# Sliding attention and output block joined into one program per layer, in a two-layer decoder step on one Trainium2 core

## Chip, cores and metric

The kernel runs on one core of one Trainium2 chip. The metric is device microseconds (us) of one launch. The engines are TensorE (PE; its weight loads are listed as PEld), VectorE (DVE), ScalarE (ACT), GpSimd (POOL) and SyncE (SP), which issues the transfers spoken of here. Each runs its own queue in order and waits on semaphores.

## What is computed

Two decoder layers over 1032 tokens: a prompt of 1024 and 8 single samples. Cut to the part that the change touches (all in fp32):

```
proj = h @ w_in
attn = sliding-window attention (window 128, 8 q heads, 2 kv heads, head dim 64, per-head sink)
rec  = HGRN2 branch (4 heads, ready before this part begins)
x   += RMSNorm_post([attn ; rec] @ w_o)
hm   = rms_norm(mem_prompt) ; mk = hm @ w_xk ; mv = hm @ w_xv      # 256 memory rows, outputs too
q    = RMSNorm_pre(x) @ w_xq                                        # queries of the cross attention
```

After it come the cross attention, its output projection and the gated MLP; before it, the input projection and the recurrence.

## The kernel before

Everything is held transposed: `xT`, `Y`, `hh` and `hl` are [128, 8, 1032] in SBUF (channel blocks by tokens). A product keeps fp32 accuracy with three matmuls per block (`mm3`, lines 257 to 259): high part of the weights by high and by low part of the activations, and low part of the weights by the high part.

**Weights** come as slabs of 128x1024 (512 KB) in a fixed order of visits (`weight_visits`). A slab is loaded into one of RR = 2 raw buffers (`w_raw`, line 225), ACT rounds it to the high part (`w_hi`, line 234), and the low part is the difference, computed by POOL (line 242) or, for 13 slabs a layer (`LOW_ON_DVE`), by DVE (line 251). High and low parts have HR = 3 slots. The load of slab m waits for the low part of slab m-2; the high part of m waits until PE has used the slab whose slot it takes. `split_hi(act, upto)` in ACT's queue issues all high parts up to a number, each with its waits, and ACT's later work stands behind them. `fits_after(v)` is the number of slabs whose slot is free once v visits are done.

**stage_window** (line 379) computes the sliding attention in 16 groups g (8 query blocks of 128, two halves of the heads). A group on PE is `scores(g+3)` (line 447), one slab of the memory's keys and values (`memory(g)`), `turn(g+1)` (transposes of the shares, line 457) and `values(g)` (line 470). DVE does `before(g+2)` (scale and mask line 588, maximum 595, small ones 596 to 598), `after(g+1)` (603 to 606), the memory's result (611) and the low part of the attention's output (580). ACT does the exponentials (526), the copy of the transposes (535), the copies of the turned memory values (557) and `split_hi`. The memory's products share bank 7 of PSUM, so each waits for the result before it.

**stage_output_query** (line 1288) is a program of its own. All engines meet between the two. It computes 24 units of the output projection (`wo`) and 24 of the queries (`xq`). A unit is one block of 128 output channels by one third of the tokens (384, 384 or 264 wide, `C3`), 24 matmuls. The order of `wo` is: for each k, thirds 0 and 1 (units 0 to 15), then third 2 for k = 7 down to 0 (units 16 to 23). ACT squares and copies each result (`evacuate`, 1478 and 1481), DVE sums the squares (1553). Of each third follow a mean on PE (1386), a root on ACT (1488), a reciprocal (1565) and `normalise` (1572) on DVE, `residual` (1579), then `high` on ACT (1494), `low` on DVE (1589), ACT's squares of the new x (1506) with their sums, and the reciprocal `scale` (1598). The two buffers `sq` make ACT wait for the sum two before. Third 0 is finished while units 16 to 23 run, thirds 1 and 2 while queries run. PE starts the first query after the copy of unit 23 (`out` >= 24). The eight samples' attention is threaded between units 1 and 16. The residual x comes back from memory in one transfer (line 1350).

## Time and profile before

| | |
|---|---|
| median of 3 runs | 3636.25 us (3630.45 to 3642.39) |
| profiled execution: its own time | 3634.12 us |
| profiled execution: span, first to last instruction | 3632.3 us |
| PE busy | 3359.7 us, 92% of the span |
| DVE busy | 2360.1 us, 65% |
| ACT busy | 1193.9 us, 33% |
| POOL busy | 677.1 us, 19% |

The part in question stands twice in the span, once for each layer: from 421.4 us to about 769.6 us in layer 0, and 1800 us later with nearly the same waits in layer 1. Busy shares are averages over stages with different limits; the order of the instructions in one stage tells more.

### The profile page before, as it was taken

The page shows a single profiled execution, that of the slowest core. Times are in us where ns is not written, and L with a number is a line of the kernel's source. Part 1 is how long each engine was busy: PE and PEld are TensorE (multiplying, and loading weights), DVE is VectorE, ACT ScalarE, POOL GpSimd, SP SyncE. Part 2 cuts the span into 40 slices and gives each one's busy share as a digit, 9 for nine tenths or more (in the row PEclk, how much of TensorE's full clock was granted, in tenths as well). Part 3 has the DMA queues.
Part 4 walks back from the last instruction along what each step waited for, and adds up shares of the span by engine and source line. Part 5 has one row for each costly group of instructions (what it writes and reads, how often), then busy time and mean ns, then how long its engine had stood idle before and what let it go on. Part 6 is the DMA issues. An engine that isn't in the chain of part 4 may idle for free. (4 is left out here: it accounts for less than half of the span.)

```text
span 3632.3 us, 49879 instructions
## 1 busy us (share of the span) xinstructions
PE 3359.7 (92%) x20860; PEld 3139.7 (86%) x20860; DVE 2360.1 (65%) x3509; ACT 1193.9 (33%) x1849; POOL 677.1 (19%) x274
## 2 busy tenths in 40 slices
PE   6999789889999999999989997798899999999997
PEld 6999768778599999999879996698786999999996
DVE  6776781824276777767787777737334676776766
ACT  5342362424232222222344424533333322212222
POOL 1111132011132122121111111311122212122120
PEclk8999899999999999999999998999999999999998
DMA  4111223212421111111121122322033111111111
GB/s 163 42 42 63 69 82 117 76 47 76 174 68 47 42 53 44 44 47 42 56 75 40 48 65 67 105 105 70 30 130 143 56 41 53 41 47 47 41 53 54
DMA packets 67807, 245.74 MB, mean 68 GB/s; under 512 B 7936, under 2 KB 19456, under 8 KB 62208
## 3 DMA queue, kind: packets, MB, share of 16 engines
q1 hardware_dynamic: 67008, 242.32, 19.6%
q8 instruction: 165, 2.70, 0.3%
q14 instruction: 58, 0.48, 0.0%
q10 hardware_dynamic: 576, 0.24, 0.0%
HBM read 214.20 MB, written 23.04 MB: 65 GB/s over the span
## 5 line engine op out<-in xcount | busy, mean ns | idle before, releaser
L257 PE MATMUL ps<-hh,w_hi 128*128 128x344 f32 (+2 forms) x4320 | 1420.6, 329 | 112.2 <-issue 26.0
L259 PE MATMUL ps<-hh,w_lo 128*128 128x344 f32 (+2 forms) x4320 | 1392.8, 322 | 0.0
L258 PE MATMUL ps<-hl,w_hi 128*128 128x344 f32 (+2 forms) x4320 | 1392.4, 322 | 0.0
L242 POOL TENSOR_TENSOR w_lo<-w_raw,w_hi 128x1024 fp32r<-128x1024 f32 x270 | 676.9, 2509 | 2892.7 <-ACT w_hi L234 2892.7
L257 PEld LDWEIGHTS ps<-hh,w_hi 128*128 128x128 f32 x4320 | 823.8, 191 | 150.1 <-issue 94.0
L258 PEld LDWEIGHTS ps<-hl,w_hi 128*128 128x128 f32 x4320 | 823.9, 191 | 2.5 <-issue 0.2
L259 PEld LDWEIGHTS ps<-hh,w_lo 128*128 128x128 f32 x4320 | 823.1, 191 | 0.0
L2540 DVE TENSOR_TENSOR Y<-Y,ps 128x344 f32<-128x344 f32 x912 | 432.9, 513 | 156.1 <-PE ps L259 156.1
L234 ACT ACTIVATE w_hi<-w_raw 128x1024 fp32r<-128x1024 f32 x296 | 310.8, 1052 | 464.1 <-PE ps L259 397.0
L2336 ACT ACTIVATE f_c<-f_u,cT 128x1032 f32<-128x1032 f32 (+1 forms) x92 | 111.4, 1213 | 669.9 <-DVE f_u L2505 663.3
L259 PE MATMUL ps<-f_ghi,w_lo 128*128 128x344 f32 x960 | 307.8, 321 | 0.0
L257 PE MATMUL ps<-f_ghi,w_hi 128*128 128x344 f32 x960 | 306.2, 319 | 0.0
L258 PE MATMUL ps<-f_glo,w_hi 128*128 128x344 f32 x960 | 306.0, 319 | 0.0
L2513 DVE SCALAR_TENSOR_TENSOR f_c<-f_u,cT,f_c 128x1024 f32<-128x1024 f32 x172 | 225.2, 1309 | 98.8 <-ACT f_c L2336 95.8
L258 PEld LDWEIGHTS ps<-f_glo,w_hi 128*128 128x128 f32 x960 | 180.8, 188 | 0.0
L259 PEld LDWEIGHTS ps<-f_ghi,w_lo 128*128 128x128 f32 x960 | 180.2, 188 | 0.0
L257 PEld LDWEIGHTS ps<-f_ghi,w_hi 128*128 128x128 f32 x960 | 180.2, 188 | 0.0
L2505 DVE TENSOR_TENSOR f_u<-ps,rs 128x1032 f32<-128x1032 f32 x86 | 105.7, 1229 | 99.1 <-PE ps L259 98.8
L2515 DVE SCALAR_TENSOR_TENSOR f_c<-f_cache,cT,f_c 128x8 f32<-128x8 f32 x172 | 123.7, 719 | 6.2
L1553 DVE TENSOR_TENSOR oq_acc<-oq_acc,oq_sq 128x384 f32<-128x384 f32 (+1 forms) x84 | 43.3, 515 | 97.1 <-ACT oq_sq L1478 92.9
L1084 DVE TENSOR_TENSOR Y<-ps,rs 128x344 f32<-128x344 f32 x120 | 60.1, 509 | 53.5 <-PE ps L259 53.3
L2352 ACT ACTIVATE f_ghi<-f_c 128x1032 fp32r<-128x1032 f32 x42 | 44.9, 1068 | 149.3 <-DVE f_c L2521 149.3
(352 smaller groups left out, 3963.8 us busy)
## 6 DMA issues: line engine op xcount, KB each, us to landing
w_raw<-in_w_stream SPq DMA_DIRECT2D x296, 512.0 KB, 3.3
out_y_cols<-xT SPq DMA_DIRECT2D x9, 1376.0 KB, 6.3
xT<-out_y_cols SPq DMA_DIRECT2D x2, 4128.0 KB, 15.7
mem_keys<-in_cache_mem_k SPq DMA_DIRECT2D x8, 1024.0 KB, 4.8
mem_values<-in_cache_mem_k SPq DMA_DIRECT2D x8, 1024.0 KB, 5.0
mem_keys<-in_cache_mem_v SPq DMA_DIRECT2D x8, 1024.0 KB, 4.8
mem_values<-in_cache_mem_v SPq DMA_DIRECT2D x8, 1024.0 KB, 5.0
xT<-in_x_cols SPq DMA_DIRECT2D x1, 4128.0 KB, 14.9
```

The costliest lines, as they stand in the source:

```text
L234: nc.scalar.activation(w_hi[:, SLOT[m], :], w_raw[:, m % RR, :], ACT.Copy).then_inc(hi_done, 1)
L242: nc.gpsimd.tensor_tensor(w_lo[:, SLOT[m], :], w_raw[:, m % RR, :], w_hi[:, SLOT[m], :].bitcast(F32), ALU.subtract).then_inc(lo_done["pool ...
L257: nc.tensor.matmul(out, whi, mhi, start=start, stop=False)
L258: nc.tensor.matmul(out, whi, mlo, start=False, stop=False)
L259: return nc.tensor.matmul(out, wlo, mhi, start=False, stop=stop)
L1084: nc.vector.tensor_tensor(dst[:, cols(c)], ps[:, u % 3, 0:CH], rs[:, cols(c)], ALU.mult)\
L2336: nc.scalar.activation(C[:, h, at], U[:, h, 2 + at.start:2 + at.stop], ACT.Identity, bias=cT[:, l, 3, col:col + 1], scale=cT[:, l, 2, col: ...
L2352: nc.scalar.activation(gh[:, j % 2, :], C[:, 1, :], ACT.Copy).then_inc(f_gh, 1)
L2505: nc.vector.tensor_tensor(tokens3(U[:, h, 2:2 + T]), ps[:, 3 * h:3 * h + 3, 0:CH], tokens3(rs[:]), ALU.mult).then_inc(f_up, 1)
L2513: dve_c(nc.vector.scalar_tensor_tensor(c[:, 0:SEQ], U[:, h, t:t + SEQ], w, c[:, 0:SEQ], ALU.mult, ALU.add))
L2515: dve_c(nc.vector.scalar_tensor_tensor(c[:, SEQ:T], ca[:, col, t, :], w, c[:, SEQ:T], ALU.mult, ALU.add))
L2540: nc.vector.tensor_tensor(y, y, b, ALU.add).then_inc(f_y, 1)
```

## The change

The two programs become one, `stage_window_output`. Its parts:

- The group loop takes two memory slabs in each of groups 0 to 7 (`memory(2g+1)` and `memory(2g+2)`, with `memory(0)` before the first turn), and one or two `wo` units in groups 8 to 15 (`UNITS_OF`), units 0 to 10 in all. Units 0 to 11 share bank 7 of PSUM.
- `wo` runs third by third: k = 0..7 for third 0, 7..0 for third 1, 0..7 for third 2. That is a third visit, and five more slabs to load and split in each layer, on POOL. The 13 slabs of `LOW_ON_DVE` stay 13: they are k = 3 to 7 of third 2 and the eight of `xq`.
- High parts are asked for one group earlier (`fits_after(visit + 1)`).
- ACT does the exponentials before the copy of the turned memory values.
- Third 0 is normalised and added to x during units 11 to 15, before unit 16; third 1 is normalised, added, squared and split while units 17 to 23 run. The squares of both new thirds are threaded between the copies of units 18 to 23 (`SQUARES`).
- x comes back in three transfers, one for each third, with slab loads between them. The two caches of the samples and the sinks are asked for after the memory's last product.

```
+    v += [(("wo", k, 2), S_WO + k) for k in range(KT)]
...
-              if VISIT[l, "wo", KT - HR, 1] < LOAD_OF.index(m) < VISIT[l, "xq", KT - 1, 1]]
+              if VISIT[l, "wo", HR - 1, 2] < LOAD_OF.index(m) < VISIT[l, "xq", KT - 1, 1]]
...
+                o_passes = [(k, 0) for k in range(KT)] + [(k, 1) for k in reversed(range(KT))] + [(k, 2) for k in range(KT)]
+                UNITS_OF = [[]] * 8 + [[0], [1], [2], [3], [4], [5, 6], [7, 8], [9, 10]]
+                MEANS = [("post", 0), ("post", 1), ("pre", 0), ("pre", 1), ("post", 2), ("pre", 2)]
...
                     def _(sp):
+                        load_slabs(sp, LOAD_OF[VISIT[l, "mem", KT + 4]])
+                        sp.wait_ge(s["t_out"], 4)
+                        sp.dma_start(io["mem_v"][l], mv).then_inc(mem_stored, 16)
+                        load_slabs(sp, LOAD_OF[VISIT[l, "wo", 1, 0]])
+                        sp.wait_ge(s["m_out"], N_MEMW)
+                        sp.dma_start(io["mem_k"][l], cT2[:]).then_inc(mem_stored, 16)
+                        sp.wait_ge(w_used, VISIT[l, "wo", 0, 0])
                         sp.dma_start(kcT[:], io["cache_win_k"][l]).then_inc(kv_in, 16)
                         sp.dma_start(vc[:], io["cache_win_v"][l]).then_inc(kv_in, 16)
...
-                        load_slabs(sp, LOAD_OF[VISIT[l, "wo", 4, 0]] + 1)
-                        sp.wait_ge(kept, 1)
-                        sp.dma_start(xT[:], io["y_cols"]).then_inc(x_in, 16)
+                        load_slabs(sp, LOAD_OF[VISIT[l, "wo", 3, 1]] + 1)
+                        sp.wait_ge(s["kv_out"], 32)
+                        sp.wait_ge(s["pv"], n)
+                        sp.wait_ge(dve_did, KEPT)
+                        for c in range(NCH):
+                            sp.dma_start(xT[:, :, cols(c)], io["y_cols"][:, :, cols(c)]).then_inc(x_in[c], 16)
+                            load_slabs(sp, LOAD_OF[VISIT[l, "wo", 3, 1]] + 2 * c + 3)
...
+                        memory(0)
+                        turn(0)
+                        for g in range(n):
+                            if g + 3 < n:
+                                scores(g + 3)
+                            if 1 <= g <= 4:
+                                turn_values(g - 1)
+                            if g < KT:
+                                memory(2 * g + 1)
+                            else:
+                                unit("wo", UNITS_OF[g][0])
+                            if g + 1 < n:
+                                turn(g + 1)
+                            if g < KT - 1:
+                                memory(2 * g + 2)
+                            for u in UNITS_OF[g][1:]:
+                                unit("wo", u)
+                            values(g)
+                            if g == n - 2:
+                                sample_scores()
+                        mean(0)
+                        unit("wo", 11)
                         sample_rows()
+                        unit("wo", 12)
                         sample_probs()
+                        unit("wo", 13)
+                        unit("wo", 14)
                         sample_values()
+                        unit("wo", 15)
                         unit("wo", 16)
                         mean(1)
+                        for u in range(17, 22):
                             unit("wo", u)
+                        mean(2)
+                        unit("wo", 22)
+                        unit("wo", 23)
+                        unit("xq", 0)
+                        mean(3)
+                        unit("xq", 1)
+                        mean(4)
+                        for u in range(2, 9):
                             unit("xq", u)
...
+                            if 1 <= g <= 4:
+                                act.wait_ge(s["t_done"], g)
...
+                            if g < KT:
+                                split_hi(act, fits_after(VISIT[l, "mem", 2 * g] + 1))
+                                if g < RH:
+                                    rows_high(g)
+                                split_hi(act, fits_after(VISIT[l, "mem", 2 * g + 1] + 1))
+                            else:
+                                if g < KT + RH:
+                                    rows_high(g - RH)
+                                evacuate(UNITS_OF[g][0])
+                                split_hi(act, fits_after(visit("wo", UNITS_OF[g][0]) + 1))
+                            if g + 1 < n:
+                                copy(g + 1)
+                            for u in UNITS_OF[g][1:]:
+                                evacuate(u)
                                 split_hi(act, fits_after(visit("wo", u) + 1))
+                        out_high(NB - 1)
+                        root(0)
+                        evacuate(11)
...
+                        root(1)
+                        high(0)
+                        for u in (17, 18):
+                            evacuate(u)
+                            split_hi(act, fits_after(visit("wo", u) + 1))
+                        squares(0, range(4))
+                        evacuate(19)
+                        split_hi(act, fits_after(visit("wo", 19) + 1))
+                        squares(0, range(4, KT))
+                        evacuate(20)
+                        split_hi(act, fits_after(visit("wo", 20) + 1))
+                        high(1)
+                        evacuate(21)
...
+                        act.wait_ge(x_ready, 2)
+                        squares(1, range(4))
+                        evacuate(22)
+                        split_hi(act, fits_after(visit("wo", 22) + 1))
+                        squares(1, range(4, KT))
+                        evacuate(23)
...
                         low_slab(0)
-                        normalise(0)
+                        normalise(1)
                         add_post(17)
                         low_slab(1)
-                        residual(0, range(0, 4))
+                        low(0, range(KT))
                         add_post(18)
                         low_slab(2)
-                        residual(0, range(4, 8))
+                        residual(1, range(4))
+                        add_pre(0, range(1, 4))
                         add_post(19)
                         low_slab(3)
-                        low(0, range(0, 4))
+                        residual(1, range(4, KT))
+                        add_pre(0, range(4, KT))
                         add_post(20)
                         low_slab(4)
-                        low(0, range(4, 8))
                         add_post(21)
                         low_slab(5)
+                        scale_of(2)
+                        low(1, range(4))
+                        add_pre(1, range(1, 4))
                         add_post(22)
+                        low(1, range(4, KT))
+                        add_pre(1, range(4, KT))
                         add_post(23)
                         low_slab(6)
-                        root(1)
-                        normalise(1)
+                        query(0)
                         low_slab(7)
-                        add_pre(0)
```

`mean`, `unit`, `evacuate`, `scores`, `turn`, `values`, `before` and `after` keep their instructions; their waits follow the new order.

## Rows read from the trace of the kernel before

**Rows 1.** The page's first line.

```profile
span 3632.3 us, 49879 instructions
```

**Rows 2.** Waits of PE over the whole span: total us, times, longest.

```profile
PE ps L457 <- DVE xT L606: 37.7, 24, 7.3
...
PE ps L257 <- DVE w_lo L251: 25.4, 12, 5.3
...
PE ps L257 <- ACT mem_values L557: 7.1, 8, 0.9
```

**Rows 3.** Windows of layer 0: busy us of each engine, granted clock, DMA share.

```profile
436.00:500.00 64.00, 56.87 (x432) 45.24 (x430) 56.57 (x87) 45.30 (x108) 16.72 (x7) 0.98 0.18 58
...
640.00:700.00 60.00, 47.48 (x278) 44.97 (x278) 51.64 (x69) 29.16 (x52) 0.00 (x0) 0.93 0.28 93
...
657.91:663.20 5.29, 5.29 (x24) 5.29 (x24) 3.89 (x7) 1.06 (x1) 0.00 (x0) 0.50 0.39 126
```

**Rows 4.** Timeline of PE, layer 0: start, us, wait before it.

```profile
556.25 0.66 PE L257 MATMUL ps<-hh,w_hi 128*128 128x384 f32 x1 [7.48 <-PEq L416]
...
657.91 0.59 PE L257 MATMUL ps<-hh,w_hi 128*128 128x264 f32 x1 [5.34 <-DVE w_lo L251]
...
664.41 0.41 PE L257 MATMUL ps<-hh,w_hi 128*128 128x384 f32 x1 [0.85 <-ACT Y L1481]
```

**Rows 5.** Timeline of POOL in the window loop.

```profile
470.89 2.39 POOL L242 TENSOR_TENSOR w_lo<-w_raw,w_hi 128x1024 fp32r<-128x1024 f32 x1 [5.18 <-ACT w_hi L234]
```

**Rows 6.** Timeline of DVE in the window loop.

```profile
468.31 1.21 DVE L588 SCALAR_TENSOR_TENSOR xT<-ps,swa_mask 128x1024 f32<-128x1024 f32 x1
...
471.01 2.29 DVE L597 TENSOR_TENSOR win_small<-sinks,win_small 128x4 f32<-128x4 f32 x1
```

**Rows 7.** Timeline of ACT: one exponential of four; its last small one.

```profile
473.54 0.51 ACT L526 ACTIVATE xT<-xT,win_small 128x256 f32<-128x256 f32 x1 [2.73 <-DVE win_small L598]
...
476.08 0.20 ACT L528 ACTIVATE win_small<-win_small 128x4 f32<-128x4 f32 x1
```

**Rows 8.** Timeline of SP between the two programs.

```profile
555.34 0.43 SPq L429 DMA_DIRECT2D out_mem_k<-mem_keys  x1
...
556.59 1.83 SPq L1345 DMA_DIRECT2D ws_values<-in_cache_win_v  x1
...
559.28 0.44 SPq L1350 DMA_DIRECT2D xT<-out_y_cols  x1
```

**Rows 9.** Issues of transfers, 500 to 575 us: KB each, us to landing.

```profile
w_raw<-in_w_stream SPq DMA_DIRECT2D x10, 512.0 KB, 3.2
...
xT<-out_y_cols SPq DMA_DIRECT2D x1, 4128.0 KB, 15.5
```

**Rows 10.** Timeline of ACT in the output projection.

```profile
609.50 0.49 ACT L1478 ACTIVATE oq_sq<-ps 128x384 f32<-128x384 f32 x1 [2.39 <-PE ps L259]
...
613.70 0.49 ACT L1478 ACTIVATE oq_sq<-ps 128x384 f32<-128x384 f32 x1 [3.33 <-PE ps L259]
...
634.08 0.39 ACT L1478 ACTIVATE oq_acc<-ps 128x264 f32<-128x264 f32 x1 [0.78 <-PE ps L259]
...
650.00 4.14 ACT L1494 ACTIVATE hh<-xT,gT 128x384 fp32r<-128x384 f32 x8
```

**Rows 11.** Timeline of DVE, unit 16 to the last query.

```profile
633.33 2.55 DVE L1565 RECIPROCAL oq_rt<-oq_rt 128x384 f32<-128x384 f32 x1 [1.72 <-ACT oq_rt L1488]
...
635.92 1.23 DVE L251 TENSOR_TENSOR w_lo<-w_raw,w_hi 128x1024 fp32r<-128x1024 f32 x1
...
637.07 3.35 DVE L1572 TENSOR_TENSOR Y<-Y,oq_rt 128x3072 f32<-128x3072 f32 x1
...
641.94 2.20 DVE L1579 SCALAR_TENSOR_TENSOR xT<-Y,gT,xT 128x384 f32<-128x384 f32 x4
...
672.62 4.53 DVE L1553 TENSOR_TENSOR oq_acc<-oq_acc,oq_sq 128x384 f32<-128x384 f32 x7
...
769.54 0.43 DVE L1608 TENSOR_TENSOR Y<-ps,rs 128x264 f32<-128x264 f32 x1 [2.35 <-PE ps L259]
```

More of the change, by code:

```diff
@@ L1360, in _, with scores @@
                     def _(pe):
+                        def scores(g):
+                            if g >= 2:
+                                pe.wait_ge(s["scores_used"], g - 1)
+                            b, jp = divmod(g, 2)
+                            k0 = P * (b - 1) if b else 0
+                            sv = scores_of(g)
+                            for j in range(2):
+                                for kv in range(NKV):
+                                    rows = slice(HD * kv, HD * kv + HD)
+                                    last = nc.tensor.matmul(sv[:, 2 * kv + j, keys_of(g):], qT[rows, 2 * jp + j, P * b:P * b + P],
+                                                            kT[rows, k0:P * (b + 1)], start=True, stop=True)
+                            last.then_inc(s["scores"], 1)
@@ new lines, in turn @@
+                        def turn(g):
+                            pe.wait_ge(s["probs"], g + 1)
+                            if g:
+                                pe.wait_ge(s["turned_copied"], g)
+                            for half in halves_of(g):
+                                for h in range(4):
+                                    last = nc.tensor.transpose(ps[:, 4 + half, P * h:P * h + P],
+                                                               S[g % 3][:, 256 * h + P * half:256 * h + P * half + P], ident[:])
+                            last.then_inc(s["turned"], 1)
@@ new lines, in values @@
+                        def values(g):
+                            b, jp = divmod(g, 2)
+                            pe.wait_ge(s["turned_copied"], g + 1)
+                            if b and jp == 0:
+                                pe.wait_ge(s["out_used"], b)
+                            pt = PT[g % 2].rearrange("p (a h q) -> p a h q", a=2, h=4)
+                            hs = halves_of(g)
+                            for i, half in enumerate(hs):
+                                for kv in range(NKV):
+                                    last = nc.tensor.matmul(ps[HD * kv:HD * kv + HD, 6, 256 * jp:256 * jp + 256],
+                                                            vtok[:, b - 1 + half, HD * kv:HD * kv + HD],
+                                                            pt[:, half, 2 * kv:2 * kv + 2].rearrange("p h q -> p (h q)"),
+                                                            start=(i == 0), stop=(i == len(hs) - 1))
+                            last.then_inc(s["pv"], 1)
@@ L1536, in _ @@
                         high(2)
-                        squares(2)
+                        squares(2, range(KT))
                         split_hi(act, fits_after(VISIT[l, "xq", 7, 0] + 1))
-                        root(4)
                         root(5)
@@ new lines, in _ @@
+                        after(0)
+                        for g in range(n):
+                            if g + 2 < n:
+                                before(g + 2)
+                            if g < KT:
+                                memory(2 * g)
+                            if g and g % 2 == 0:
+                                out_low(g // 2 - 1)
+                            if g + 1 < n:
+                                after(g + 1)
+                            if 1 <= g <= RH:
+                                rows_low(g - 1)
+                            elif KT < g <= KT + RH:
+                                rows_low(g - RH - 1)
+                            if g < KT:
+                                memory(2 * g + 1)
+                            for u in UNITS_OF[g]:
+                                if u % KT:
+                                    add_post(u)
@@ L1622, in _ @@
+                        out_low(NB - 1)
+                        dve.wait_ge(pe_did, ROWS)
                         sc = HD ** -0.5
@@ L1680, in _ @@
-                        query(0)
+                        scale_of(3)
                         query(1)
-                        residual(1, range(0, 4))
+                        normalise(4)
+                        query(2)
                         low_slab(9)
-                        query(2)
-                        residual(1, range(4, 8))
+                        residual(2, range(4))
                         query(3)
                         low_slab(10)
-                        root(3)
```

695 lines of the change are left out of this document (292 added, 403 removed).

## The prediction, made before the changed kernel was run

> **What bounds the kernel now.** I read the page first, then PE's waits, then windows of layer 0, then the timelines of each queue around the waits. The profiled execution took 3634.12 us of its own time, 1.8 us more than its span [rows 1]; it lies 2.1 us under the median 3636.25. PE is busy for 92% of the span, so a change like this can win only PE's waits. Those that it touches [rows 2, 4], halved for one layer: the turns wait for the shares, 18.9 us, of which 7.3 at the first turn and 11.5 in the loop; 3.6 behind the copies of the memory values; 7.5 between the two programs; 12.7 for low parts made by DVE. Two windows say why [rows 3]. In 436 to 500 us DVE works 56.57 of 64 us, as much as PE: the loop is at DVE's limit. In 640 to 700 us DVE works 51.64 of 60 us and PE only 47.48: here DVE sets the pace.
>
> **The clock.** After the wait of 5.34 us PE ran at half clock (0.50, the 1.2 GHz level) for 5.3 us [rows 3, 4], which costs 2.65 us. I charge this wherever a wait is longer than that and PE sets the pace afterwards; the wait of 7.5 between the programs pays it too.
>
> **Step 1, what goes, per layer.** The meeting of all engines: 7.5 + 2.6 = 10.1 us. The turns' waits in the loop, 11.5: a group of the first eight gives PE two memory products in place of one. PE's own work in a group: 432 matmuls in 64 us at 44 a group are 9.8 groups, 56.87 / 9.8 = 5.8 us each [rows 3]; a unit of 384 columns is 4.2 us by the spacing of its squares [rows 10], a memory product of 256 columns 4.2 x 256/384 = 2.8; so 3.0 are the group's own and the new group has 3.0 + 5.6 = 8.6 us. DVE's part grows only by one more result. The copies' waits, 3.6. The first memory product ahead of the first turn: about 1.2, since it waits only for the memory's low parts. Sum: -26.4 us.
>
> **Step 2, what comes in the window loop and units 0 to 15.**
> (a) In groups 1 to 4 ACT now does exponentials before it copies the turned values, and the product behind waits. Exponentials last 2.7 us [rows 7] and start when DVE has the maxima, after one 1.2 us pass, one about as long and three small ones [rows 6]. So the copy, some 0.5 like a unit's [rows 10], is ready about 0.4 + 3.1 + 2.7 + 0.5 = 6.7 us after a product, when PE has the group's 3.0, a product of 2.8 and four transposes, about 0.6, behind it, 6.4: wait 0.3. If POOL's low part stands in the way of DVE's small instruction, add 2: the one at 471.01 took 2.29 us and ended with POOL's [rows 5, 6]. Two slabs a group make that frequent. I take 1.5 of 0.3 to 2.3, four times: 6 us (1 to 9).
> (b) SyncE's queue has slab k=1 of the output projection behind the memory's last result, the store of the keys, and the caches. From the store to what follows the caches SyncE took 3.9 us [rows 8]. Count from the end of the last memory product: result 0.5, queue 3.9, landing 3.2 alone [rows 9], or about 4.6 behind 2 MB of store and caches at 4.2 MB in 15.5 us and the rest; so 7.6 to 9. ACT, a group ahead, stands at this slab and the next before the copy of turn 8, so that both high parts (1.9), copy (1.0), the attention's output high and low (1.1) and DVE's shares (1.6) follow: 13.2 to 14.6. PE comes to the turn that wants the shares after 3.0 + 4.2 = 7.2. Wait 6 to 8.7; I take 8.7, as the caches really are in front, and half clock after it: 11.3 us.
> (c) The same at slab k=2 of third 1: it is issued after the last `values`, behind 1.6 MB of x, and lands 7 us later. ACT stands at it before the last attention output and the first root. High part, output high and low: 9.5. PE has a mean and unit 11, 5.1, then unit 12 waits 4.4; with half clock 7.0 (0 to 8).
> (d) Units 0 to 10 share one bank, with one group's own work between: its copy, 0.9, is hidden behind 3.0, unless ACT is late. A group with one unit has 7.2 us of PE against DVE's same 7. I take 0.3 a group, 2.3 us. The five more slabs (ACT 1.06, POOL 2.4 each) lie in these gaps; a further price would be the shared port, in (a).
> Sum of 2: +26.6. Steps 1 and 2 cancel: +0.2 (range -9 to +8).
>
> **Step 3, third 2 of the projection.** Count from the end of unit 16, T. PE has a mean 0.6 and five units of 4.2 x 264/384 = 2.9: 15.1 us, then `mean(2)`, which wants all sums of new third 0. DVE's queue before that: the root is there at T+3.4 (evacuation 0.7, high part 1.0, mean and root 1.7, as before the reciprocal at 633.33), then reciprocal 2.55, normalise 3.35, low parts of third 0 4.3, three slabs after the first 3.5, half of `residual` twice 4.3, seven sums of squares 4.5, three more sums 1.2 [rows 11]. End: T+27. PE waits 12.
> Then ACT: copy of unit 20, a high part, `high(1)` 4.1 [rows 10], unit 21's copy; 6.4 in all, and DVE goes on: slab, `scale` 2.55, low 4.3, seven sums 4.5 less what ACT runs ahead, two sums, and ACT copies unit 23, which stands behind its last squares. I count 12.6 to 14. So T+46 (to 48) for query 0, against 15.1 + 0.6 + 5.8 = 21.5 of PE's work. Before, from unit 16's end at 634.0 to the first query at 664.4 [rows 4, 10]: 30.4. Thus +15.6 us. The half clock is inside these waits, for DVE sets the pace.
>
> **Step 4, the queries.** Before: 664.4 to 769.5, 105.1 us [rows 4, 11]. PE's work: 16 x 4.2 + 8 x 2.9 + means 1.6 = 92.1. After, DVE has less left (`scale` twice, root and normalise of third 2, residual and low of third 2, eight sums, seven slabs, nine results: 31 us) under nine queries of 38 us. I leave 6 us of waits for the order, half of the 13, and 2.6 of half clock: 100.8. -4.3; between 0 and -10.
>
> **The sum.** +0.2 + 15.6 - 4.3 = +11.5 a layer, twice: 3634.1 + 23.0 = 3657.1 us, +0.6%; the 2.1 us between this execution and the median lie inside the range. Everything else of the span keeps its instructions.
>
> **A rule beside the rows.** At 471.01 DVE ended with POOL [rows 5, 6]. The Trainium skill, "SBUF — State Buffer", Who interferes with whom, says that DVE with two SBUF inputs and POOL exclude each other for whole instructions. The trace agrees. By it alone two slabs a group could cost DVE 4.8 us in each of eight groups, and the time would be rival 3's.
>
> **Rivals.**
> 1. Faster: DVE's queue in third 2 is not the limit (place: between unit 16 and query 0). For it: before, the same engines finished third 0 there with one long wait of 5.3. Against: DVE's list above, 27 us before `mean(2)` alone. If the stretch takes 30.4 as before, the sum is 0.2 - 4.3 = -4.1 a layer, and with (b) at 6 + 2.6, its low end, -6.8: 3634.1 - 13.6 = 3620 us. It decides once the stretch is under some 34 us. The Trainium skill, "Perfetto Trace Analysis", Optimization Strategy, says that interleaving regimes with different busiest engines may help; by it this rival would hold. The loop does interleave so, and third 2 is the opposite.
> 2. The slabs of (b) and (c) cost half of their waits, 4 and 2 us, and no half clock: 6 in place of 18.3. Step 3 stays: -0.8 a layer, 3632.5 us. No change. For it: 3.2 us of landing alone. Against: SyncE's order, which nothing shortens.
> 3. The port: DVE loses 2.4 us for each slab in the eight groups with two slabs and is the bound: 56.57 / 9.8 = 5.8 [rows 3] + 4.8 = 10.6 against PE's 8.6, 16 us in eight groups less the 6 that (a) has: +10 on the forecast, 3657 + 20 = 3677 us. Against: in 436 to 500 us seven slabs by POOL (16.72 us) left DVE 7 us of room [rows 3], and part of its passes read PSUM.
> 4. The change does not do what it says: the meeting stays, as a chain of the same waits. That is (b), and is in the forecast.
>
> **Chances.** Forecast, with its own range 3645 to 3672: 0.58. Rival 1: 0.15. Rival 2: 0.13. Rival 3: 0.10. 0.04 for something else. A difference under 0.3%, 11 us, can hardly be told from none. Faster takes rival 1; same takes rival 2 and the forecast's lowest end; the rest is slower: 0.16, 0.15, 0.69. The range that holds 8 in 10 leaves a tail of rival 1 and of rival 3: 3624 to 3684.
>
> **What the profile after would show.** Step 1: no wait of 7.5 before unit 0, waits of turns in groups 1 to 8 under 1 us in all. 2a: four waits of 0.3 to 2.3 for `mem_values`. 2b: one wait of 6 to 9 at turn 9, ACT before it waiting for a transfer. 2c: about 4 before unit 12. Step 3: PE's busy share from unit 17 to query 0 under 55%, with DVE near 90%. Step 4: waits under 9 us in the queries. I would be wrong if ACT passes slab k=1 without a wait, or if query 0 starts under 34 us after unit 16.

## The result, and the profile after

The changed kernel took 3669.22 us (median of 4, 3663.34 to 3674.97) against 3634.62 us for the kernel before beside it: a ratio of 1.0097, interval 1.0084 to 1.011, or 34.6 us more. The forecast was 3657 us, 23 us more, in a range of 3624 to 3684. The profiled execution below is the longest of the four (3674.97 us, span 3673.1), 5.8 us above their median, so sums over its trace come out larger by that.

The waits of TensorE after; the columns are as in [rows 2]:

```profile
PE ps L258 <- issue: 60.4, 44, 11.4
PE ps L1174 <- DVE xT L1539: 22.6, 6, 10.1
...
PE ps L258 <- ACT mem_values L1437: 15.7, 8, 2.4
PE ps L258 <- DVE w_lo L252: 15.4, 6, 3.3
...
PE ps L258 <- DVE hl L1513: 12.9, 2, 6.5
PE ps L1254 <- DVE oq_acc L1559: 12.4, 2, 6.2
...
PE ps L2051 <- PEq L1119: 8.8, 2, 4.4
```

The turns' 24 waits of 37.7 us are 6 of 22.6, and of these two are 10 us long. The copies of the memory values cost 15.7 us instead of 7.1. A new wait for `hl` (line 1513, the attention output's low part) stands before unit 12, one for `oq_acc` before `mean(2)`, and what the profile calls "issue" has a new longest of 11.4. Where they lie is in the timeline of TensorE after, layer 0; it answers to [rows 4]:

```profile
451.78 0.36 PE L258 MATMUL ps<-mem_hi,w_hi 128*128 128x256 f32 x1 [2.37 <-ACT mem_values L1437]
...
476.50 0.36 PE L258 MATMUL ps<-mem_hi,w_hi 128*128 128x256 f32 x1 [0.91 <-ACT mem_values L1437]
...
537.15 1.12 PE L1174 MATMUL ps<-ident,xT 128*128 128x128 f32 x4 [10.10 <-DVE xT L1539]
...
619.37 0.66 PE L258 MATMUL ps<-hh,w_hi 128*128 128x384 f32 x1 [6.47 <-DVE hl L1513]
...
670.72 1.01 PE L1254 MATMUL ps<-oq_acc,ones 128*128 128x384 f32 x1 [6.20 <-DVE oq_acc L1559]
...
690.32 0.66 PE L258 MATMUL ps<-hh,w_hi 128*128 128x384 f32 x1 [11.31 <-issue]
...
797.72 0.76 PE L2051 MATMUL ps<-mem_keys,Y 128*128 128x256 f32 x1 [4.41 <-PEq L1119]
```

From top to bottom: two of the four waits for the copies; turn 9; unit 12; `mean(2)`; query 0; the cross attention. Windows of the changed kernel, layer 0 (busy us of PE, PEld, DVE, ACT, POOL; then the granted clock):

```profile
448.00:460.00 12.00, 9.28 (x64) 8.57 (x60) 6.11 (x11) 6.43 (x14) 4.76 (x2) 0.86 0.29 94
460.00:470.00 10.00, 7.75 (x50) 6.75 (x50) 4.26 (x11) 5.81 (x14) 2.39 (x2) 0.83 0.29 85
...
537.00:543.00 6.00, 5.85 (x30) 4.02 (x31) 5.79 (x10) 4.08 (x10) 2.35 (x1) 0.67 0.38 132
619.00:625.00 6.00, 5.63 (x23) 5.66 (x24) 2.91 (x12) 5.07 (x9) 3.84 (x2) 0.68 0.66 224
643.00:670.00 27.00, 17.14 (x122) 16.31 (x120) 23.57 (x31) 15.81 (x30) 0.00 (x0) 0.89 0.24 78
670.00:690.00 20.00, 8.29 (x50) 7.47 (x50) 14.71 (x23) 13.35 (x28) 0.00 (x0) 0.76 0.16 53
690.00:696.00 6.00, 5.68 (x22) 5.71 (x23) 1.68 (x3) 1.17 (x2) 0.00 (x0) 0.62 0.23 87
```

Each long wait is followed by some us at a clock between the two levels of 1.2 and 2.4 GHz on average (0.67, 0.68, 0.62), and the loop's short waits by 0.86 and 0.83. In third 2 TensorE works 25.4 of 47 us while VectorE works 38.3.

To see in which stretch the time went, I put four events of a layer on one scale. Zero is SyncE's load of `mem_cols`, with which the window's program begins; "mem" is the time between the first and the last result of a memory product, "last mem" when the last one comes, "unit 16" is ScalarE's first work on its result, "cross" the first matmul of the cross attention (us, layer 0 / layer 1; the edits follow below):

| kernel | mem | last mem | unit 16 done | cross |
|---|---|---|---|---|
| before | 107.1 / 107.1 | 126.5 / 126.4 | 212.8 / 212.6 | 356.7 / 356.2 |
| after | 81.3 / 81.3 | 98.2 / 98.0 | 221.4 / 221.0 | 376.2 / 376.1 |
| e1 | 79.6 / 81.0 | 96.4 / 96.9 | 208.4 / 208.7 | 362.9 / 363.2 |
| e2 | 79.6 / 77.7 | 96.5 / 93.5 | 213.6 / 208.3 | 367.7 / 361.6 |
| e3 | 73.4 / 73.1 | 90.3 / 89.7 | 214.7 / 213.4 | 369.4 / 368.8 |
| e5 | 77.7 / 79.5 | 93.7 / 96.3 | 218.4 / 218.5 | 340.4 / 341.1 |
| e6 | 73.1 / 73.1 | 89.0 / 89.0 | 194.8 / 193.4 | 347.9 / 347.4 |
| e7 | 73.5 / 73.1 | 90.3 / 89.8 | 194.8 / 194.2 | 316.3 / 315.6 |
| e8 | 77.8 / 77.8 | 93.6 / 93.6 | 218.3 / 215.6 | 377.3 / 374.3 |

In layer 0 of the kernels before and after, the change loses 8.6 us up to the end of unit 16 and 10.8 behind it. The loss behind it is +17.0 from unit 16 to query 0 (47.4 us, 642.93 to 690.32, against 30.4), -2.1 for the queries (103.0 against 105.1) and -4.1 at the meeting before the cross attention (4.41 us; the kernel before waits 8.55 there). After, e1, e2, e5 and e8 have the same code between the two memory events and differ by up to 3.6 us there. That much is the clock of one execution: TensorE's 546 matmuls of this stretch take 69.5 to 72.9 us in these ten layers, while its idle time in it is nearly the same, 8.2 to 8.7 us. The 81.3 of the changed kernel's profiled execution is 2.0 above the mean of the ten, 79.3.

### The profile page after: what moved, and what is told of

Same layout as the page of the kernel before. It is cut to its first block and busy times, and to the rows that moved or that the text cites. A ratio compares the mean times of both kernels' runs of the same rounds, so it can differ in the third digit from the quotient of the medians.

```text
span 3673.1 us, 49999 instructions
## 1 busy us (share of the span) xinstructions
PE 3375.6 (92%) x20860; PEld 3158.3 (86%) x20860; DVE 2347.9 (64%) x3517; ACT 1205.8 (33%) x1871; POOL 697.9 (19%) x284
## 3 DMA queue, kind: packets, MB, share of 16 engines
q1 hardware_dynamic: 74400, 247.56, 19.9%
## 5 line engine op out<-in xcount | busy, mean ns | idle before, releaser
L243 POOL TENSOR_TENSOR w_lo<-w_raw,w_hi 128x1024 fp32r<-128x1024 f32 x280 | 697.7, 2494 | 2912.7 <-ACT w_hi L235 2912.7
L235 ACT ACTIVATE w_hi<-w_raw 128x1024 fp32r<-128x1024 f32 x306 | 321.9, 1053 | 575.4 <-PE ps L260 452.9
L258 PE MATMUL ps<-mem_hi,w_hi 128*128 128x256 f32 x256 | 80.9, 316 | 28.0 <-ACT mem_values L1437 15.7
```

The source lines that it names most:

```text
L235: nc.scalar.activation(w_hi[:, SLOT[m], :], w_raw[:, m % RR, :], ACT.Copy).then_inc(hi_done, 1)
L243: nc.gpsimd.tensor_tensor(w_lo[:, SLOT[m], :], w_raw[:, m % RR, :], w_hi[:, SLOT[m], :].bitcast(F32), ALU.subtract).then_inc(lo_done["pool ...
L258: nc.tensor.matmul(out, whi, mhi, start=start, stop=False)
```

## The experiments

Eight kernels were run. Gains are given as ratios to the kernel before beside them; a difference of two ratios times 3634.6 us is the gain in us. For the changed kernel the ratio is 1.0097.

**e1, slabs before the store.** One line of SyncE:

```diff
-                        load_slabs(sp, LOAD_OF[VISIT[l, "wo", 1, 0]])
+                        load_slabs(sp, LOAD_OF[VISIT[l, "wo", 3, 0]])
                         sp.wait_ge(s["m_out"], N_MEMW)
                         sp.dma_start(io["mem_k"][l], cT2[:]).then_inc(mem_stored, 16)
```

> The changed kernel with one edit: SyncE issues slabs k=1 and k=2 of the output projection's third 0 before it stores the memory's keys and loads the caches, instead of after. In the changed kernel's layer 0 the slab is issued at 523.12 us, behind the store (520.18) and the caches, although POOL had made its buffer free at about 513; ACT stands at it for 10.91 us and TensorE waits 10.10 us at turn 9. Theory (SyncE's order costs it): the slab lands before the last memory product is done, the wait of 10.10 us at turn 9 goes in both layers, and with it about 2 us of half clock after it: 20 to 26 us less than the changed kernel's 3669, so 3643 to 3649. Rival (the slab is late whoever is first, because a group ahead is too early for two raw buffers): a wait of 5 us or more stays at turn 9, and the time is 3657 or above.

Measured: 3647.98 us, ratio 1.0037 (1.0023 to 1.005): 22 us less than the changed kernel. SyncE's timeline of the changed kernel, with ScalarE's wait for the slab behind it:

```profile
520.18 0.34 SPq L1133 DMA_DIRECT2D out_mem_k<-mem_keys  x1
...
522.00 1.07 SPq L1137 DMA_DIRECT2D ws_sinks<-in_attn_sinks  x1
523.12 1.01 SPq L226 DMA_DIRECT2D w_raw<-in_w_stream  x2
...
529.82 1.06 ACT L235 ACTIVATE w_hi<-w_raw 128x1024 fp32r<-128x1024 f32 x1 [10.91 <-DMA w_raw<-in_w_stream]
```

and the same queue in e1, with the window that had a clock of 0.67 in the changed kernel (e1's turn 9 runs earlier, at 521.95, and its clock is 1.00 in each window of 6 us from 515 to 545):

```profile
501.37 9.37 SPq L226 DMA_DIRECT2D w_raw<-in_w_stream  x3
514.86 0.34 SPq L1133 DMA_DIRECT2D out_mem_k<-mem_keys  x1
...
537.00:543.00 6.00, 6.00 (x42) 4.93 (x41) 4.85 (x10) 3.95 (x9) 2.40 (x1) 1.00 0.01 3
```

In e1 the three slab loads are issued before the store, and the six waits of turns are 3.2 us in all, the longest 1.0, where they were 22.6 and 10.1. So the slab was late because of its place in the queue, and the rival is out. From the last memory result to unit 16 e1 needs 112.0 / 111.8 us where the changed kernel needs 123.2 / 123.0: 11.2 us a layer, of which 9.7 are the turns' waits and the rest, by difference, the clock.

**e2, slabs before x.** SyncE loads two slabs of third 1 more before it waits for the last values and loads x:

```diff
-                        load_slabs(sp, LOAD_OF[VISIT[l, "wo", 3, 1]] + 1)
+                        load_slabs(sp, LOAD_OF[VISIT[l, "wo", 3, 1]] + 3)
...
-                            load_slabs(sp, LOAD_OF[VISIT[l, "wo", 3, 1]] + 2 * c + 3)
+                            load_slabs(sp, LOAD_OF[VISIT[l, "wo", 3, 1]] + 2 * c + 5)
```

> The changed kernel with one edit: two slabs of third 1 more are issued before SyncE waits for the last values and loads x, so that no slab is queued behind x (1.5 MB each for the first two thirds). In the changed kernel's layer 0 ACT stands at such a slab for 9.47 us until 616.96, and TensorE waits 6.47 us before unit 12, with a granted clock of 0.68 in the 6 us after it. Theory (the slab is late because it is behind x in the queue): the wait of 6.5 us goes in both layers with up to 3 us of slow clock: 13 to 19 us less than 3669, so 3650 to 3656. Rival (third 2 is set by VectorE's queue, which starts no earlier): the wait goes from unit 12 but returns before the first query, and the time stays within 4 us of 3669.

Measured: 3655.89 us, ratio 1.0053 (1.004 to 1.0066): 16 us less. TensorE no longer waits for `hl` of line 1513. In the changed kernel that wait came by way of ScalarE, which stood at the slab:

```profile
616.96 1.06 ACT L235 ACTIVATE w_hi<-w_raw 128x1024 fp32r<-128x1024 f32 x1 [9.47 <-DMA w_raw<-in_w_stream]
```

From the last memory result to unit 16 it needs 117.1 / 114.8 us, 7.2 a layer less than the changed kernel. From unit 16 to the cross attention it needs 154.1 / 153.3 against 154.8 / 155.1: the gain does not return in third 2, against the rival.

**e3, copies first.** In ScalarE's loop the copy of the turned memory values moves from behind `exps(g + 2)` to ahead of it and of `out_high`:

```diff
+                            if 1 <= g <= 4:
+                                act.wait_ge(s["t_done"], g)
+                                nc.scalar.activation(mv..., ps[:, 7, :]..., ACT.Copy).then_inc(s["t_out"], 1)
                             if g and g % 2 == 0:
                                 out_high(g // 2 - 1)
                             if g + 2 < n:
                                 exps(g + 2)
```

> The changed kernel with one edit: in groups 1 to 4 ACT copies the turned memory values before it does the exponentials, as the kernel before does, not after them. The changed kernel has four waits of TensorE there, 2.37, 2.25, 0.91 and 2.25 us = 7.8 us in layer 0, and the granted clock is 0.83 to 0.86 in 448 to 470 us and 0.50 in 490 to 493 us. Theory (ACT's order, and short waits one behind another bring the clock down too): the four waits are about 0.9 each as before, 4 us less, and the clock is 1.00 there, 3 to 5 us less: 7 to 9 a layer, 14 to 18 in all, so 3651 to 3655. Rival A (only the waits count; the slow clock has another cause): 8 us less, 3661, with the clock as it was. Rival B (the exponentials now come later, so that the turns wait for the shares instead): no gain, and waits of the turns in groups 1 to 5 of 0.5 us or more.

Measured: 3659.92 us, ratio 1.0061 (1.0048 to 1.0075): 13 us less by the ratios, 9.3 by the medians. The intervals are too wide to tell the theory's 14 from rival A's 8; the trace tells more. Waits of TensorE and windows of e3:

```profile
PE ps L258 <- ACT mem_values L1433: 6.2, 8, 0.8
...
448.00:460.00 12.00, 10.86 (x89) 9.69 (x88) 9.12 (x14) 7.15 (x16) 6.25 (x4) 1.00 0.28 89
460.00:470.00 10.00, 8.64 (x70) 7.46 (x70) 7.92 (x12) 6.13 (x15) 3.77 (x2) 1.00 0.32 105
```

The eight waits go from 15.7 to 6.2 us, 4.75 a layer; the clock is 1.00 where it was 0.86 and 0.83, and no waits of turns come in (22.2 in 6, against 22.6), so rival B is out. The stretch between the memory results is 73.2 us, against a mean of 79.3 over the ten layers with the other order (table): 6.1 us a layer. How much of it is clock can be read from the 546 matmuls that every one of these stretches has; here are the changed kernel, e5 (which has its order) and e3:

```profile
438.41:519.73 81.32, 72.87 (x546) 64.08 (x545) 50.59 (x82) 46.35 (x105) 33.26 (x14) 0.94 0.27 91
```

```profile
435.34:513.07 77.73, 69.56 (x546) 60.86 (x545) 50.31 (x82) 46.34 (x105) 33.27 (x14) 0.98 0.28 96
```

```profile
441.99:515.39 73.40, 68.60 (x546) 59.55 (x545) 55.19 (x81) 45.87 (x105) 33.11 (x14) 1.00 0.31 101
```

TensorE is idle for 4.8 us in e3 and for 8.3 on the mean of the ten: 3.5 less, since about 1.1 of the 4.75 come back as waits for a memory result. Its matmuls take 68.4 us against a mean of 71.0: 2.6 are clock. Both parts of the theory hold, and rival A is out by the trace, but the clock's part was not the same each time, 1.1 to 4.4 us a layer, with a mean below the 3 to 5 I expected.

**e4, clears earlier.** This is the kernel before with one line moved:

```diff
-                        load_slabs(sp, fits_after(end) + RR)
-                        sp.wait_ge(mem_stored, 32 * (l + 1))
-                        clear(sp, "hg", "w")
+                        load_slabs(sp, fits_after(end) + RR - 2)
+                        clear(sp, "hg", "w")
+                        load_slabs(sp, fits_after(end) + RR)
+                        sp.wait_ge(mem_stored, 32 * (l + 1))
```

> The kernel before with one edit: SyncE clears the 65 semaphores of the earlier programs before it issues the last two slabs of the output block's program, not after them. The changed kernel waits 4.41 us before the cross attention, the kernel before 8.55 us; nothing else there differs but where semaphores are cleared, and SyncE took 2.58 us from the load ahead of 43 clears to the store behind them in the changed kernel. Theory (the clears are on the path at the meeting of engines, 0.06 us each): 65 x 0.06 = 3.9 us a layer less, the wait before the cross attention about 4.5, and 3634.6 - 8 = 3627 us. Rival (the longer wait is something else, for example the weights' high part): no change, 3634, and the wait stays above 8 us.

Measured: 3625.25 us, ratio 0.9973 (0.9962 to 0.9985): 9.4 us less than the kernel before. The timeline of the kernel before shows SyncE's last load and then TensorE's wait to the cross attention:

```profile
773.10 0.33 SPq L225 DMA_DIRECT2D w_raw<-in_w_stream  x1
...
778.06 0.76 PE L2024 MATMUL ps<-mem_keys,Y 128*128 128x256 f32 x1 [8.55 <-PEq L1341]
```

In e4 the same wait is

```profile
771.02 1.19 PE L2025 MATMUL ps<-mem_keys,Y 128*128 128x256 f32 x2 [4.41 <-PEq L1341]
```

In the 4.6 us between SyncE's last load (773.10 + 0.33) and 778.06 nothing of SyncE is in the trace: clears leave no record. In the changed kernel 44 clears lie between these two rows of SyncE:

```profile
421.56 0.34 SPq L1122 DMA_DIRECT2D mem_values<-in_mem_cols  x1
424.48 0.34 SPq L1126 DMA_DIRECT2D out_win_k<-xT  x1
```

424.48 - 421.56 - 0.34 is 2.58 us for 44, 0.06 us each; the kernel before makes 66 at its meeting (by one each more than I had counted for the expectation). The wait is 4.1 us shorter with nothing moved but the clears, and the rival is out. So the 4.1 us a layer that the changed kernel wins at this meeting come from where it clears semaphores, not from joining the programs.

**e5, sums after queries.** Third 2 of the changed kernel in another order. TensorE, and the order of sums and means:

```diff
-                MEANS = [("post", 0), ("post", 1), ("pre", 0), ("pre", 1), ("post", 2), ("pre", 2)]
+                MEANS = [("post", 0), ("post", 1), ("pre", 0), ("post", 2), ("pre", 1), ("pre", 2)]
+                SQUARES = [(kind, c, i) for kind in ("post", "pre") for c in range(NCH) for i in range(KT)]
...
-                                pe.wait_ge(out, 24)
+                                pe.wait_ge(out, min(24, 21 + u))
...
-                        for u in range(17, 22):
-                            unit("wo", u)
-                        mean(2)
...
+                        for u in range(17, 24):
+                            unit("wo", u)
+                        for u in range(24):
+                            if u in (3, 4, 10, 12):
+                                mean({3: 2, 4: 3, 10: 4, 12: 5}[u])
+                            unit("xq", u)
```

ScalarE evacuates units 17 to 23 in a row and then does the squares of third 0, roots 2 and 3, `high(1)`, `high(2)`, the squares of third 1, root 4, the squares of third 2 and root 5, with the slabs' high parts between them. VectorE's queue up to query 8 is now: slab 0, `normalise(1)`, slabs 1 and 2, the sums of units 17 to 23 with `low(0)`, slabs 3 to 6 and the first half of `residual(1)` between them, slab 7, the sums of new third 0, the second half of `residual(1)`, slabs 8 and 9, `scale_of(2)`, queries 0 and 1, slab 10, `normalise(3)`, slab 11, queries 2 to 4, slab 12, query 5, `residual(2)`, `low(1)`, `low(2)`, the sums of third 1, queries 6 and 7, the sums of third 2, `scale_of(4)`, query 8, `scale_of(5)`. The operations are the same ones.

> The changed kernel with the order of third 2 changed and nothing else: VectorE makes the sums of squares of the new thirds, their roots' reciprocals and the low parts of third 1 after what the first query wants; ScalarE evacuates units 17 to 23 before it squares the new thirds; TensorE does its means between queries 3 and 12, and a query waits only for the evacuation of its own bank. In the changed kernel 47.4 us lie between the end of unit 16 and query 0, against 21.5 us of TensorE's work, and VectorE works 38.3 of them. Theory (VectorE's queue in third 2 sets the pace, and about 20 us of its work are not wanted by the first query): query 0 starts 23 to 30 us after unit 16, some of it comes back as waits between queries 4 and 9, and the time falls by 10 to 20 us a layer: 3629 to 3649. Rival A (VectorE's whole work up to query 9 sets the end): the first query comes early, but the last query is less than 5 us a layer earlier, 3659 or above. Rival B (the chain through ScalarE, not VectorE's work, holds query 0): it starts 40 us or more after unit 16.

Measured: 3604.56 us, ratio 0.992 (0.9904 to 0.9936): 64 us less than the changed kernel, where I had expected 20 to 40, and less than the kernel before. The first row is TensorE's query 0 in e5 (unit 16 was done at 637.84), the others are windows of e5, unit 16 to query 0 and query 0 to the cross attention; the next fence has the same two windows of the changed kernel:

```profile
660.58 0.44 PE L258 MATMUL ps<-hh,w_hi 128*128 128x384 f32 x1
...
637.84:660.50 22.66, 21.16 (x170) 20.49 (x168) 18.68 (x21) 16.42 (x31) 0.00 (x0) 1.00 0.34 116
660.50:759.80 99.30, 93.91 (x585) 91.98 (x585) 57.32 (x93) 35.97 (x62) 19.07 (x8) 0.99 0.24 80
```

```profile
642.93:690.30 47.37, 25.50 (x172) 23.80 (x171) 38.48 (x54) 29.53 (x59) 0.00 (x0) 0.83 0.21 67
690.30:797.70 107.40, 97.83 (x582) 96.59 (x583) 38.33 (x59) 22.31 (x34) 19.08 (x8) 0.94 0.21 69
```

Query 0 starts 22.7 us after unit 16 instead of 47.4, and both rivals are out. VectorE does the same work in all, 76.0 against 76.8 us, but only 18.7 us of it before query 0 instead of 38.5. TensorE has 6.9 us without work instead of 31.4, and its own matmuls take 115.1 us instead of 123.3, because the clock stays up: of the 32.8 us a layer, 24.6 are waits and 8.3 the clock. The edit reorders three queues at once and lets the first queries wait for fewer evacuations; no run moves VectorE's queue alone, so what each part is worth stays open.

**e6, three orders.** The edits of e1, e2 and e3 together.

> The changed kernel with the edits of e1, e2 and e3 together. Theory (three waits at three places that don't hide one another): the gains add, 21.2 + 13.3 + 9.3 = 43.8 us, 3625. Rival (VectorE or ScalarE then sets the pace between the places, so that part of one gain is lost in another): 3635 or above, with new waits of TensorE between turn 9 and unit 12.

Measured: 3616.86 us, ratio 0.9955 (0.9942 to 0.9968): 52 us less than the changed kernel; the three alone gave 22 + 16 + 13 = 51 by the same reckoning. They add within their intervals, and the rival is out. The median is below the 3625 expected because that sum took the medians' smaller differences, 43.8. The joined program now reaches unit 16 at 194.8 / 193.4 us, 18.6 a layer earlier than the kernel before.

**e7, four orders.** The edits of e1, e2, e3 and e5 together.

> The changed kernel with the edits of e1, e2, e3 and e5 together. Theory: the gain of e5 (20 to 40 us) comes on top of the 44 of the other three: 3585 to 3605, below the kernel before (3634.6) by 0.8 to 1.4%. Rival (with units 0 to 16 done earlier, VectorE and POOL are what the queries wait for): the gain of e5 is halved or lost, 3610 to 3625.

Measured: 3551.98 us, ratio 0.9778 (0.9765 to 0.9792): 2.2% faster than the kernel before, 116 us less than the changed kernel; e5 and e6 add up to 64 + 52. It is better than even the theory had it, since e5 gave more than the 20 to 40 us I had put down. VectorE and POOL do not become what the queries wait for: from unit 16 to the cross attention it needs 121.5 / 121.4 us, e5 122.0 / 122.6.

**e8, five lows twice.** In the changed kernel VectorE makes the low parts of the five slabs of third 2 twice:

```diff
                         def low_slab(i):
+                            if i < 5:
+                                m = LOW_ON_DVE[len(LOW_ON_DVE) // DEPTH * l + i]
+                                dve.wait_ge(hi_done, m + 1)
+                                dve_c(nc.vector.tensor_tensor(w_lo[:, SLOT[m], :], w_raw[:, m % RR, :],
+                                                              w_hi[:, SLOT[m], :].bitcast(F32), ALU.subtract))
                             split_lo_dve(dve, LOW_ON_DVE[len(LOW_ON_DVE) // DEPTH * l + i] + 1)
```

> The changed kernel with VectorE making the low parts of the five slabs of third 2 twice (the same values written again, 1.2 us each): a price put on VectorE's queue between units 17 and 23. Theory (VectorE sets the pace there): 5 x 1.2 = 6 us later at query 0 in each layer, 12 us in all, 3681. Rival A (ScalarE's chain sets it and VectorE has room, 9 of 47 us idle): under 4 us in all, 3669 to 3673. Rival B (the extra work keeps POOL off the shared port too): over 16 us, 3685 or more.

Measured: 3678.19 us, ratio 1.0124 (1.0106 to 1.0142): 10 us more than the changed kernel. The two intervals overlap (the changed kernel's ends at 1.011), so the times alone can't tell the theory's 12 from rival A's 4, or from no change; the trace does. Query 0 of e8:

```profile
695.74 0.66 PE L258 MATMUL ps<-hh,w_hi 128*128 128x384 f32 x1 [11.47 <-issue]
```

Unit 16 was done at 644.07, so it starts 51.7 us after it, 4.3 more than in the changed kernel for 6.2 us of added work; in layer 1 it is 4.3 too. VectorE's queue sets the pace there, with about 2 us of slack where it waits for ScalarE (its wait of 3.09 us for the square of unit 21 is 1.83 in e8). Rival A's 4 us in all would be 2 a layer, and rival B's 16 would be 8.

## Why the prediction was right, and where its sizes were off

The direction and the mechanism were right: what the joined program wins in the loop it loses again at three places, and the order of third 2 makes it slower. By the table the change costs 19.5 and 19.9 us a layer where I had 11.5; by the medians it is 17.3. That the sum came this near is in part luck: the steps were 8.3, 1.4 and 2.2 us too low, and 4.1 came back at a place that had no term.

**Steps 1 and 2, up to unit 16: +0.2 forecast, +8.5 measured.** The windows from SyncE's load of `mem_cols` to unit 16 have the same 1259 matmuls in each kernel. Before:

```profile
421.30:634.08 212.78, 182.70 (x1259) 159.85 (x1260) 120.36 (x198) 108.05 (x246) 51.16 (x21) 0.94 0.27 93
```

after:

```profile
421.56:642.93 221.37, 186.33 (x1259) 164.31 (x1260) 123.65 (x211) 113.32 (x255) 61.79 (x26) 0.91 0.30 101
```

and e6:

```profile
424.64:619.44 194.80, 179.30 (x1259) 158.01 (x1260) 129.26 (x211) 112.60 (x255) 62.68 (x26) 0.96 0.31 110
```

On the mean of both layers TensorE idles 30.0 us before, 34.6 after and 15.6 in e6, and its matmuls take 182.7, 186.6 and 178.5. So the +8.5 are +4.6 of waits and +3.9 of clock. My terms were 23.8 us of waits gone (7.5 + 11.5 + 3.6 + 1.2) and 21.4 new ones (6 + 8.7 + 4.4 + 2.3), so -2.4, and +2.6 of clock. The waits were 7.0 too low and the clock 1.3.
- 2(b), the slab behind the store: 11.3 forecast, 11.2 by e1. 2(c), the slab behind x: 7.0 forecast, 7.2 by e2. SyncE's order is their cause, as I had it. That the sizes agree is luck in part: the waits were 10.1 and 6.5 us where I had 8.7 and 4.4, and the clock behind them cost less than the 2.6 that I charged for each.
- 2(a) was under-sized: 6 forecast. The four waits are 7.8 us in layer 0 and e3 adds 2.6 of clock: 10.4. I had 1.5 for each wait out of 0.3 to 2.3, and three of the four are 2.25 to 2.37. I also charged slow clock only behind waits of over 5 us; the loop's windows show 0.86 and 0.83 behind waits of 2.3.
- The three long ones have two causes. In group 1 it is the small maximum, as I feared: VectorE's and POOL's timelines of the changed kernel (group 1, then groups 2 and 3)

```profile
443.24 4.71 POOL L243 TENSOR_TENSOR w_lo<-w_raw,w_hi 128x1024 fp32r<-128x1024 f32 x2 [25.80 <-ACT w_hi L235]
```

```profile
445.94 2.03 DVE L1529 TENSOR_TENSOR win_small<-win_small,sinks 128x4 f32<-128x4 f32 x1
...
459.27 0.77 DVE L1529 TENSOR_TENSOR win_small<-win_small,sinks 128x4 f32<-128x4 f32 x1
...
471.91 0.78 DVE L1529 TENSOR_TENSOR win_small<-win_small,sinks 128x4 f32<-128x4 f32 x1
```

  It takes 2.03 us and ends at 447.97, with POOL's second slab (447.95), and the product behind it waits 2.37. In group 3 it takes 0.78, and the wait is 0.91. But in groups 2 and 4 it takes no longer (0.77 and 0.76), and the waits are 2.25 all the same. There ScalarE stands at `out_high` before the exponentials, and that waits for TensorE's `values`:

```profile
460.74 0.60 ACT L1370 ACTIVATE hh<-ps 128x512 fp32r<-128x512 f32 x1 [2.28 <-PE ps L1187]
...
484.37 0.60 ACT L1370 ACTIVATE hh<-ps 128x512 fp32r<-128x512 f32 x1 [2.72 <-PE ps L1187]
```

  so that the exponentials start at 461.23 and 484.87, 0.8 and 1.2 us after VectorE's last small instruction; in group 3 they follow it at once. In group 2 TensorE's own `values` are 0.4 us shorter as well. Layer 1 has the same four. I had no term for `out_high` standing first; e3 moves the copy ahead of both, and all four waits are 0.78.
- The Trainium skill, "SBUF — State Buffer", Who interferes with whom, says that a VectorE instruction with two SBUF inputs contends with a GpSimd instruction that reads SBUF, under an exclusive lock. This trace agrees again: the maximum takes 0.16 us at its shortest, and in each of groups 1 to 7 of layer 0 it lasts 0.76 to 2.36 us and ends with a POOL pass. But one small instruction a group is held and not 2.4 us for each slab, so rival 3 did not come.
- Step 1 was too large. At unit 16 the joined program of e6 is 18.6 us ahead of the kernel before (14.4 of waits, 4.2 of clock), where my terms without the three places give 23.8 - 3.1 (the copies' waits that stay) - 2.3 = 18.4 of waits and 2.6 of clock. The missing 4.0 us of waits had no term: in e6's layer 0 turns still wait 1.5 us, products and transposes 1.7 for memory results and a sample's transpose 0.8. The 2.2 us that units wait for a copy of the bank they share are the 2.3 of 2(d).
- I counted 44 matmuls in a group of the loop, and there are 48; the group's own work is then 3.5 us and not 3.0, and the new group 9.1 and not 8.6. The memory results of the later groups come every 8.95 us (501.81, 510.76, 519.73). The sum does not use the 8.6. The 3.0 stands in the estimates of 2(a) and 2(b), whose waits would have been 0.5 us lower with 3.5.

**Step 3: +15.6 forecast, +17.0 measured.** Right in cause and nearly in size. `mean(2)` ran at 670.72, T + 27.8 for T + 27; query 0 at T + 47.4 for T + 46. e8 shows that VectorE's queue sets the pace, and e5 that the order of third 2 cost it, not the amount of VectorE's work.

**Step 4: -4.3 forecast, -2.1 measured.** The queries' waits were 5.2 us where I had 6. Their matmuls take 97.8 us, and 93.9 in e5 at a clock of 0.99: the slow clock is 3.9 us where I had 2.6, and the work itself 1.8 us more than my 92.1.

**What had no term:** the meeting before the cross attention. I wrote that everything else keeps its instructions, but the diff moves the clears of 44 semaphores to the start of the program and of 22 behind the meeting. It is worth -4.1 us a layer (e4). Without this unpriced gain the forecast would have been 8 us further off.

**Of what the profile was to show:** no wait of 7.5 before unit 0, and no waits of turns in groups 1 to 8: right. Four waits of 0.3 to 2.3 for `mem_values`: right but for one of 2.37. One of 6 to 9 at turn 9: it is 10.1. About 4 before unit 12: it is 6.5. TensorE's share from unit 17 to query 0 under 55%: 25.5 of 47.4, 54%. VectorE near 90%: it is 81%, with a hole of 3.1 us in the middle, where it waits for ScalarE's square of unit 21 behind `high(1)`. Waits under 9 us in the queries: right, 107.4 - 97.8 less the 4.4 of the meeting is 5.2.

**The rivals.** Rival 1 needed under 34 us from unit 16 to query 0, and the changed kernel has 47. But its rule has a point: the Trainium skill, "Perfetto Trace Analysis", Optimization Strategy, says that interleaving regimes with different busiest engines may improve performance. e5 does so in third 2 (VectorE works 18.7 of the 22.7 us before query 0 and goes on under the queries, with TensorE busy for 115.1 of the 122.0 us), and it wins 64 us. Rival 2 fails by e1 and e2. Rival 3 wanted a group of 10.6 us with VectorE as its bound; it is 8.95, and VectorE works 50.6 of the 81.3 us between the memory results. Rival 4, the meeting as a chain of waits, is e1's wait.

## What to carry to other kernels

Where programs are joined, look first at the queue that serves all of them: a weight slab issued behind a store, or behind a large load for later, holds up the engine that converts slabs a group ahead, and everything behind that engine. Where one engine is the limit of a stretch, ask which of its operations the next matmul wants, and put the rest under the matmuls that have room for it: here the same 76 us of VectorE's work cost 32.8 us a layer more in one order of the queues than in the other. The joined program as it was written is slower than the kernel before; with e5's order alone it is 0.8% faster, with all four 2.2%. How much of that needs the joining is not shown: some 9 us come from where semaphores are cleared, which e4 wins without it, and no run puts e5's order into the two programs of the kernel before. With the first three orders alone (e6, 0.9942 to 0.9968) it cannot be told from e4 (0.9962 to 0.9985).

## What the runs showed of the hardware that I had not expected

- The granted clock falls behind short waits too, though not behind each: 0.86 and 0.83 in a loop where TensorE waits 0.9 to 2.4 us once in each group, 1.00 with waits of 0.8 or less in the same loop. The rows below are e5's, which has the changed kernel's order in this loop: behind the wait of 2.37 the window is at 1.00, and the next one, behind a wait of 2.25, at 0.83.

```profile
448.56 0.36 PE L258 MATMUL ps<-mem_hi,w_hi 128*128 128x256 f32 x1 [2.37 <-ACT mem_values L1425]
...
448.00:460.00 12.00, 9.19 (x73) 8.12 (x74) 6.84 (x12) 7.63 (x17) 4.78 (x2) 1.00 0.26 89
460.00:470.00 10.00, 10.00 (x72) 9.17 (x72) 5.57 (x10) 4.84 (x10) 4.77 (x2) 0.83 0.27 93
```

- Over third 2 and the queries the same matmuls took 123.3 us in one order and 115.1 in another: a quarter of what the better order won is clock.
- Clearing a semaphore costs SyncE 0.06 us and leaves no row; with 66 of them moved away from a meeting, TensorE waits 4.1 us less there.
